# Router of a mixture of experts computed from the unscaled residual, with the normalisation applied later

## The reference, cut to what matters

```python
def rms_norm(x, g):
    xf = x.astype(jnp.float32)
    y = xf * lax.rsqrt(jnp.mean(xf * xf, axis=-1, keepdims=True) + EPS)
    return (y * g.astype(jnp.float32)).astype(x.dtype)

def moe_swiglu(h, w_router, wg, wu, wd):
    xt = h.reshape(-1, d)
    logits = (xt @ w_router).astype(jnp.float32)
    top_v, top_i = lax.top_k(logits, TOP_K)
    gates = jax.nn.softmax(top_v, axis=-1)
    comb = jnp.sum(jax.nn.one_hot(top_i, N_EXPERTS, dtype=jnp.float32) * gates[..., None], axis=1)
    y = jnp.zeros_like(xt)
    for e in range(N_EXPERTS):
        y = y + comb[:, e:e + 1] * swiglu(xt, wg[e], wu[e], wd[e])
    return y.reshape(bsz, s, d)

# layer 1 of the first block
x = x + hybrid_mixer(rms_norm(x, norm_mix[1]), ...)
x = x + moe_swiglu(rms_norm(x, norm_ffn[1]), ...)
```

## Time and profile before

| what | us |
|---|---|
| three runs | 1823.79, 1824.40, 1828.91 |
| median | 1824.40 |
| profiled execution, its time | 1823.32 |
| profiled execution, its span in the trace | 1821.1 |
| TensorE busy | 1771.0 (97%) |
| VectorE busy | 1437.4 (79%) |
| ScalarE busy | 1165.8 (64%) |
| GpSimd busy | 30.6 (2%) |
| mean granted clock of TensorE, as a share of full | 0.988 |

### The profile page before, as it was taken

One profiled execution on the slowest core, in us unless ns is written; L12 is line 12 of the kernel. 1 busy time (PEld: TensorE's weight loads), 2 busy tenths in 40 slices (PEclk: granted clock), 3 DMA queues, 4 the chain that ended last, 5 costly groups with the idle time before them and its releaser, 6 DMA issues.

```text
span 1821.1 us, 26224 instructions
## 1 busy us (share of the span) xinstructions
PE 1771.0 (97%) x9177; PEld 1499.7 (82%) x9177; DVE 1437.4 (79%) x1661; ACT 1165.8 (64%) x1410; POOL 30.6 (2%) x45
## 2 busy tenths in 40 slices
PE   7999999996999999999999999999999999999998
PEld 7988888896788888888888888888888797878986
DVE  7864444797799998999989999999999887636455
ACT  5554343463677778777777787777777656544554
POOL 0000000000000000000000000000000001000000
PEclk9999999997999999999999999999999999999999
DMA  9555555444699999999999999989999643324520
GB/s 336 168 173 196 184 185 187 158 157 144 231 376 381 349 384 329 359 383 348 385 330 353 387 370 361 378 316 379 378 347 386 234 162 116 139 88 153 176 93 35
DMA packets 210541, 482.44 MB, mean 265 GB/s; under 512 B 13269, under 2 KB 14500, under 8 KB 210484
## 3 DMA queue, kind: packets, MB, share of 16 engines
q1 hardware_dynamic: 209840, 480.02, 73.9%
q10 hardware_dynamic: 644, 1.63, 0.2%
HBM read 480.57 MB, written 1.05 MB: 264 GB/s over the span
## 4 chain that ended last, share of the span: by engine, by line
PE 92%; DVE 5%; ACT 1%; issue 1%; DMA 0%; POOL 0%; DVEq 0%; POOLq 0%; ACTq 0%
PE ps L1733 84%; PE ps L2018 1%; DVE wlo L939 1%; PE ps L1982 1%; DVE arena L1401 1%; DVE arena L930 1%; PE ps L2239 0%; PE ps L1816 0%; PE ps L2028 0%; PE ps L2029 0%; ACT whi L432 0%; PE ps L2162 0%; PE ps L1872 0%; PE ps L2235 0%; PE ps L2176 0%
## 5 line engine op out<-in xcount | busy, mean ns | idle before, releaser
L939 DVE TENSOR_TENSOR wlo<-raw,whi 128x1024 fp32r<-128x1024 f32 x910 | 1068.5, 1221 | 256.3 <-ACT whi L432 256.0
L432 ACT ACTIVATE whi<-raw 128x1024 fp32r<-128x1024 f32 x910 | 912.7, 1053 | 460.1 <-PE ps L1733 458.3
L1733 PE MATMUL ps<-whi,ya 128*128 128x512 f32 x2272 | 727.9, 393 | 5.9 <-DVE ya L930 4.7
L1733 PEld LDWEIGHTS ps<-whi,ya 128*128 128x128 f32 x2272 | 427.7, 188 | 94.9 <-issue 6.8
L1733 PE MATMUL ps<-wlo,ya 128*128 128x512 f32 x1136 | 443.2, 390 | 0.0
L1733 PE MATMUL ps<-whi,yh 128*128 128x512 f32 x896 | 285.4, 390 | 0.0
L1733 PEld LDWEIGHTS ps<-wlo,ya 128*128 128x128 f32 x1136 | 214.1, 188 | 42.6
L1733 PEld LDWEIGHTS ps<-whi,yh 128*128 128x128 f32 x896 | 168.2, 188 | 35.4 <-issue 0.7
L1733 PE MATMUL ps<-hhi,whi 128*128 128x256 f32 x656 | 188.0, 287 | 2.7 <-DVE hlo L1007 2.2
L1733 PE MATMUL ps<-hhi,wlo 128*128 128x256 f32 x656 | 185.5, 283 | 0.0
L1733 PE MATMUL ps<-hlo,whi 128*128 128x256 f32 x656 | 185.5, 283 | 0.0
(11 more groups left out here) (342 smaller groups left out, 1189.2 us busy)
## 6 DMA issues: line engine op xcount, KB each, us to landing
raw<-in_moe_w_gate SPq DMA_DIRECT2D x112, 1024.0 KB, 5.8
raw<-in_moe_w_up SPq DMA_DIRECT2D x112, 1024.0 KB, 6.6
raw<-in_moe_w_down SPq DMA_DIRECT2D x112, 1024.0 KB, 6.4
raw<-in_even_w_in SPq DMA_DIRECT2D x21, 1024.0 KB, 5.1
raw<-in_w_in SPq DMA_DIRECT2D x20, 1024.0 KB, 6.0
raw<-in_odd_w_in SPq DMA_DIRECT2D x16, 1024.0 KB, 5.2
raw<-in_ffn_w_gate SPq DMA_DIRECT2D x14, 1024.0 KB, 5.1
raw<-in_ffn_w_up SPq DMA_DIRECT2D x14, 1024.0 KB, 5.1
```

The source lines that it names most:

```text
L432: act.activation(hi_of(u)[:, n], raw[:, c % RAW, n], ACT.Copy).then_inc(w_hi, 1)
L939: dve.tensor_tensor(lo_of(u)[:, n], raw[:, c % RAW, n], hi_of(u)[:, n].bitcast(F32), ALU.subtract).then_inc(w_lo, 1)
L1733: ins = pe.matmul(o, s, m, start=first and n == 0, stop=last and n == 2, skip_group_check=True)
```

## The change

- **Residual and transposes.** The mixer's last unit becomes `rows_end`, so the unscaled residual is transposed as its quarters arrive. `hTf` is now `X` transposed times the norm weight, without the token factor; its eight copies signal one by one, and the router's matmuls take them in this order. The logits lack the token factor, which is positive for each token and so leaves its ranking alone; the exponential gets it as its scale.
- **Squares.** ScalarE squares token tile 1 as well, in two halves; GpSimd adds them before its factor.
- **Norm weight early, token factor at the split.** GpSimd multiplies tile 0 of `X` by `BG` and VectorE tile 1. ScalarE's rounding has the token factor as its scale, and VectorE's lower half has it as a multiplier, each tile by itself (`low_rows`). The gain vector is loaded in the mixer already.
- **Gather.** The one-hot columns of the first pair come straight from `T16`; the gather goes token tile by token tile and starts with tile 0; its third and fourth bank are 1 and 7 instead of 0 and 1, so the split of its second half has two instructions of 512 columns. The expert loop's first matmuls wait for one half of it at a time.
- **Overflow list.** Its operations move to GpSimd (`overflow`), where each sum over eight is a tree of three additions; `tab` gets its first four entries from there. VectorE waits for it (`r_over`) in the second step of each pair, SyncE only if there is overflow. The clearing of buffers moves to GpSimd too, some of it into the mixer, the rank mask `LTM` into the kernel's start.
- **Order.** The weight split that stood before the router on ScalarE and VectorE (`after(U_LRU1 + 13)`) stands behind the exponential and the gates. Fourteen transposes without a use (`keep_busy`) follow the router and the counting on TensorE.

```diff
 # GpSimd
             def rstd(k, n, scale):
...
+                if k == 3:
+                    link(pool.tensor_tensor(ssq[:, 1:2], ssq[:, 1:2], ssq[:, 2:3], ALU.add))
...
+            def overflow():
+
+                pool.memset(JC, 0.0)
+                pool.wait_ge(sem("r_log"), 1)
+                pool.memset(yh[:, 1536:2048].bitcast(F32), 0.0).then_inc(sem("m_st"), 1)
...
+                pool.wait_ge(sem("r_comb"), 1)
+                G = GT3[:, 0, :].rearrange("p (e f) -> p e f", e=NE)
+                link(pool.tensor_tensor(G, OV.unsqueeze(1).to_broadcast([P, NE, NE]), LTM[:, :].rearrange("p (e f) -> p e f", e=NE), ALU.mult))
+                def total(o, x):
+
+                    link(pool.tensor_tensor(x(0, 4), x(0, 4), x(4, 8), ALU.add))
+                    link(pool.tensor_tensor(x(0, 2), x(0, 2), x(2, 4), ALU.add))
+                    link(pool.tensor_tensor(o, x(0, 1), x(1, 2), ALU.add))
+
+                total(OVR.unsqueeze(2), lambda u, v: G[:, :, u:v])
+                for m in range(3):
+                    link(pool.tensor_scalar(SEL, OVR, float(m), None, ALU.is_equal))
...
+                pool.tensor_copy(tab[:, 0:4], TF[:, 0:4]).then_inc(sem("r_over"), 1)
...
+                if k == 3:
+                    pool.wait_ge(sem("lru_gate"), 4)
+                    pool.memset(yb[:, 0:2048].bitcast(F32), 0.0)
+                    pool.wait_ge(s_bg, 16)
+                    pool.wait_ge(sem("x_half"), 10)
+                    pool.tensor_tensor(HTOK[:, 0, :], X[:, 0, :], BG, ALU.mult).then_inc(sem("x_gain0"), 1)
 # ScalarE
             norm_ssq(3, X[:, 0, :])
-            after(U_LRU1 + 13)
-            load_gain(a["norm_ffn"][1])
-            turn(3, gcol(0, C_NFFN + 8), full=hTf)
-            act.wait_ge(sem("htok"), 1)
-            act.activation(hhi[:, :], HTOK.rearrange("p i n -> p (i n)"), ACT.Copy).then_inc(sem("htok_hi"), 1)
+            for h in range(2):
+                act.wait_ge(sem("x_half"), 11 + h)
+                act.wait_ge(sem("ssq_a"), 4 + h)
+                act.activation(A[:, 7200:7712], X[:, 1, 512 * h:512 * (h + 1)], ACT.Square, accum_out=ssq[:, 1 + h:2 + h]).then_inc(sem("ssq_a"), 1)
+            for c in (0, 1, 4, 5):
+                act.wait_ge(sem("c_turned"), KD * 2 + (c | 1) + 1)
+                act.activation(hTf[:, c, :], ...).then_inc(sem("r_fa"), 1)
+            act.wait_ge(sem("rstd"), 4)
+            for i in range(NT):
+                act.wait_ge(sem(f"x_gain{i}"), 1)
+                act.activation(hhi[:, 1024 * i:1024 * (i + 1)], HTOK[:, i, :], ACT.Copy, scale=rst[:, i:i + 1]).then_inc(sem("htok_hi"), 1)
             load_gain(a["norm_final"])
             act.wait_ge(sem("r_sub"), 1)
+            for i in range(NT):
+                ins = act.activation(EX[:, i, :], EX[:, i, :], ACT.Exp, scale=rst[:, i:i + 1])
+            ins.then_inc(sem("r_exp"), 1)
+            after(U_LRU1 + 13)
 # VectorE
-            residual(U_LRU1 + 13)
-            ssq_of(3, X[:, 1, :], HTOK[:, 1, :])
-            normed(3, X)
-            after(U_LRU1 + 13)
-            turn(3, gcol(0, C_NFFN + 8), full=hTf)
+            residual_halves(2, U_LRU1 + 13)
+            for c in (2, 3, 6, 7):
+                dve.wait_ge(sem("c_turned"), KD * 2 + (c | 1) + 1)
+                dve.tensor_scalar(hTf[:, c, :], ...).then_inc(sem("r_fv"), 1)
             dve.wait_ge(s_bg, 16)
+            dve.wait_ge(sem("x_half"), 12)
+            tt(HTOK[:, 1, :], X[:, 1, :], BG, ALU.mult).then_inc(sem("x_gain1"), 1)
...
             tt(EX, L, MX.unsqueeze(2).to_broadcast([P, NT, NE]), ALU.subtract).then_inc(sem("r_sub"), 1)
+            dve.wait_ge(sem("rstd"), 4)
+            low_rows(0)
             dve.wait_ge(sem("r_ch"), 1)
...
             link(dve.scalar_tensor_tensor(T16, R[:, 0:2, :], 1.0, CH, ALU.add, ALU.mult))
+            for i in range(NT):
+                for e in range(2):
+                    ins = dve.tensor_scalar(SR[:, i, P * e:P * (e + 1)], iot[:, :], 1.0, T16[:, i, e:e + 1], ALU.add, ALU.is_equal)
+            ins.then_inc(sem("m_s"), 1)
+            low_rows(1)
+            link(dve.tensor_scalar(OV, R[:, 2, :], float(P), None, ALU.is_gt))
...
+            dve.tensor_copy(tab[:, 4:6], TF[:, 4:6]).then_inc(sem("tab_ready"), 1)
+            dve.tensor_scalar(POS[:, :, 0:NE], T16, -1.0, None, ALU.add)
+            dve.wait_ge(sem("r_exp"), 1)
...
+            after(U_LRU1 + 13)
...
                 if place is not None:
+                    dve.wait_ge(sem("r_over"), 1)
                     dve.wait_ge(sem("m_str"), place + 1)
 # TensorE
+            for k in range(KD):
+                pe.wait_ge(sem("r_fv" if k & 2 else "r_fa"), 2 * (k // 4) + k % 2 + 1)
+                for i in range(NT):
+                    ins = pe.matmul(ps[:, 6 + i, 0:NE], hTf[:, k, P * i:P * (i + 1)], WR[:, k, :], start=k == 0, stop=k == KD - 1)
             ins.then_inc(sem("r_log"), 1)
+            keep_busy(3, 8)
             pe.wait_ge(sem("r_ch"), 1)
...
+            keep_busy(3, 6)
...
+            def gather(k, fresh=False):
+
+                pe.wait_ge(sem("m_s"), k + 1)
+                for i in range(NT):
+                    if fresh:
+                        pe.wait_ge(sem("htok_lo"), i + 1)
+                    for c in range(KD):
+                        o = ps[:, (5, 6, 1, 7)[c // 2], S * (c % 2):S * (c % 2 + 1)]
+                        pe.matmul(o, TKh[:, i, P * c:P * (c + 1)], SR[:, i, :], start=i == 0 and c % 2 == 0, stop=False)
+                        ins = pe.matmul(o, TKl[:, i, P * c:P * (c + 1)], SR[:, i, :], start=False, stop=i == 1 and c % 2 == 1)
+                        if i == 1 and c % 4 == 3:
+                            ins.then_inc(sem("m_gth"), 1)
```

243 lines of the change are left out of this document (107 added, 136 removed).

## The result

Four runs of the changed kernel took 1,804.12, 1,809.89, 1,804.40 and 1,809.85 us, median 1,807.12; four of the kernel before 1,823.79, 1,828.91, 1,824.40 and 1,829.18, median 1,826.66. The ratio is 0.990, with a 95% interval of 0.9885 to 0.9915. Both kernels show two levels some 5 us apart; lowest against lowest the change is worth 19.7 us, and highest against highest 19.3. The kernel before was run again beside the experiments: of 36 further runs (two far slower ones left out) only three lay on its upper level, and the medians were 1,823.57 to 1,823.91. Its median of four here is thus high, and against those medians the median of the changed kernel is 16.5 to 16.8 us lower, and not 19.5. Which level a run fell in moves a median by some 5 us, so sizes are read from the traces.

The account below looks back on a forecast made before the run. TensorE holds 92% of the chain, with five waits for VectorE, 17.7 us, before the experts. Eleven steps started the experts 17.9 us earlier: 1,823.3 - 17.9 = 1,805.4 profiled, 1,806.5 on the median; range 1,802 to 1,812.

Parts of the forecast that it names:

- Steps 1 and 2: Last projection and transposes: last projection matmul 0.8 us later, at 422.7; squares and first router copy done at 424.9.
- Step 3: Router on TensorE: 32 passes at full clock, 0.11 us each, 3.5 in all, to 428.4; bound 7.0 at half clock.
- Step 5: Lower half of tile 0 on VectorE beside TensorE's position counts: both needed, half clock costing 0.9 us, full clock nothing.
- Step 10: Register loads of the job count on VectorE, behind the weight split: 1.6 us, to 440.2.
- Step 11: Lower half of the first gathered half, 1.15 us, and 0.15 to TensorE: experts start at 441.5.
- The gather at nothing: First gather costs 0 us, covered by split and register loads; without these two, up to 2.8 us.
- rival B: Clock falls in router or counts, gather ends late, experts start at full clock: 1,808.5 us, down to 1,805; chance 0.25.
- D: Rival: half clock throughout, experts' start included, plus the loop's 1.6 us: 1,812.5 us; chance 0.08.
- C: Rival: full clock throughout, at the experts' start too: 1,804.1 us; chance 0.12.
- E: Rival: overflow list comes late, GpSimd's port held throughout, a stall of 9.4 us: 1,815.9 us; chance 0.05.
- F: Rival: late overflow list stalls VectorE 33 us in the first pair's second step, about 1,840 us, slower; chance 0.03.
- G: Rival: work only moved, path before the experts not shortened, time within 5 us of before; chance 0.02.

Follow-up runs that it names:

- halves_early: Kernel after with the weight split moved ahead of the router's logits and the first gather ordered by column halves: median 1,808.32 us of five runs.
- split_early: Kernel after with the weight split moved ahead, on VectorE in front of the router's logits: median 1,806.95 us of four runs.
- list_twice: Kernel after with GpSimd making the overflow list's sums twice, same result: median 1,813.47 us of seven runs.
- scaled_first: Kernel after with the router computed from the scaled residual again, which is transposed a second time: median 1,811.16 us of four runs.
- list_dve: Kernel after with the overflow list summed by VectorE again, between gates and weight split: median 1,811.18 us of four runs.
- before_list: Kernel before with only the overflow list moved to GpSimd and waited for in a pair's second step: median 1,823.24 us of ten runs, ratio 0.9993.
- no_keep_busy: Kernel after without the fourteen transposes that nobody reads: median 1,806.85 us of six runs.
- both_halves: Kernel after with the experts' first pair waiting for both rounded halves of the gathered tokens again: median 1,806.81 us of five runs.
- dense_halves_early: halves_early with unread 512-column matmuls replacing the unread transposes, and one more before each of the router's eight column groups: median 1,805.89 us of five runs.

## Why the prediction was right

The forecast for the profiled execution was 1,805.4 and it took 1,804.1; on the median, 1,806.5 against 1,807.1. The result lies in the range of 1,802 to 1,812, and a gain of over 0.3% had been given 0.93. The path was the forecast one: VectorE's queue of split, register loads and subtraction releases the experts. That the numbers agree so closely is in part luck. The start came 0.4 us late because two errors inside cancelled, a half clock in router and counts (1.9 too little) and the register loads (1.4 too much); the 2.1 us of clock at the experts' start came on top, so the first scatter group gained 19.6 us and the span 19.1, not 17.9. The medians agree to 0.6 us only because both stand at a mixture of the two levels: they differ by 19.5.

- **Steps 1 and 2** held: last projection matmul 422.60 (422.7), first router matmul 424.89 (424.9).
- **Step 3** took full clock for all of the router. It fell at about 427.9 (0.91 over the window of 3.6 us); 32 passes took 4.3 us and not 3.5. Up to the fall they kept the price of 0.11 each (26 in 2.9 us) that the step had taken from a wider matmul; the clock was what failed. Its bound of 7.0 was far.
- **Step 4** held: 2.0 us.
- **Step 5** named both cases; it was the half clock. The sum had taken the other case, full clock. The counts took 2.3 us, as the half-clock case says, and VectorE waited 1.00 us for them; the fold came at 433.79, 1.0 behind the later of the two cases, which is mostly what step 3 had lost. From here the sum is 1.7 to 1.9 late: one-hot ended 434.88 (433.0), table 437.17 (435.3), split 440.33 (438.6).
- **Step 10** is the term that was mis-sized: 1.6 for the register loads in series behind the split, measured 0.2. The 1.6 of the kernel before are a gap in which VectorE has nothing else in execution. Beside a split of 2.4 us they are hidden, as their rows in the trace and, by contrast, the 1.40 in halves_early show. That gave back 1.4.
- **Step 11** as forecast, at 441.92 against 441.5.
- **The gather at nothing** held, though barely. The prediction's case at half clock had its first part ready at 439.8; it was 440.53, and VectorE waited 0.2 for it. split_early shows that it sits right behind the queue.
- **The clock at the experts' start** was assumed at half, as before; it was full, 2.1 us (2.4 were named). The tie that the text drew between a slow gather and a fast start is what happened: the case lies at rival B in its mechanism, with less lost in router and counts than B's 4.4. D is excluded by the same row, C by the windows at 0.50.
- **The list**: start 438.08 (436.3), end 468.3 (465), VectorE at its wait at 481.2 (482.9), no stall. E and F didn't happen; list_twice shows that the place is right; the price, one for one in E, is 6.0 us of TensorE for 8.1 of VectorE, and 8.0 with the clock. G falls with scaled_first and list_dve.
- **The signs.** Six held: the start, the order of VectorE's queue, TensorE's waits (0.9 us besides the last), the list's end before 470, no idle VectorE at 483, and 72 expert matmuls in 16.4 us (16.6 for the first 72). One didn't: the router's passes at 3.5 us and clock 1.00. The half clock was named as a sign of B or D, and it was B's.
- **The gather's new order in the loop** was put at 0 with a bound of 1.6; it took 0.1.

How the 17.5 us divide, by undoing one part of the kernel after: router on the scaled residual 5.6, list on VectorE 5.9, waiting for both halves 1.4, the transposes nobody reads 1.1, 14.0 together, each from one profiled execution. The rest (the turned quarters in the projection, the norm weight and the lower halves moved out of the ranks' way, three copies and memsets) wasn't tried by itself. These prices hold one at a time; before_list shows that they don't simply add.

**A better version?** halves_early starts the experts 0.83 us earlier than the kernel after and keeps 0.9 at their end. Its lowest run is 1.35 us below (1,802.77 against 1,804.12), but the medians (1,808.32 of five and 1,807.12 of four) are set by which level the runs fell in. It is ahead in the trace and not shown faster in the time.

## What to carry to other kernels

When a stretch is limited by one engine's queue, ask for each instruction in it what the engine's sequencer can do meanwhile: a register load behind a long instruction was free here, and taking the long one away brings the load back. An engine that feeds the same consumer in parallel (here the gather) caps the gain of every such edit, so cost both at each clock level. And shortening a wait of TensorE can pay twice, or cost twice: behind 1.5 us of waiting the experts' first 5 us ran at full clock, behind 3.0 us some 3 of them ran at half, and behind 4.7 us the first 4.6.

## What was not expected of the hardware

- The clock after an idle stretch before the experts: full for the first 5 us in all eleven executions with up to 2.5 us (among them 1.0, 1.2, 1.5 and 2.5 in halves_early, no_keep_busy, after and before_list), half from the start after 4.7 and 7.0 us (before, list_dve), and after 3.0 us (both_halves) full at first and half from 0.7 us on. Yet in the next stage the same 0.80 us are followed by either.
- The clock fell in the middle of continuous work too: inside the router after, with TensorE busy in 3.60 of 3.60 us, 0.7 us into the experts in both_halves, and in dense_halves_early behind 5 us of busy TensorE with matmuls of 512 columns among the small ones.
- One fall of the clock in a place that no edit touched is worth 5.8 us in a run, over six times the largest gain of all edits on top of the change (0.9).
- GpSimd's first addition of 128x32 took 1.11 us beside VectorE's split with two SBUF inputs and 0.25 without it (after, halves_early).
